# Gate, running sums and scaled level forms made during the odd projection, and the gated scan as a pipeline over heads and levels

## The chip, the cores and the metric

The kernel runs on one core of a Trainium2 chip. The metric is the device time of one execution in microseconds (us). Before the change it was 3591.56 us, the median of three runs (3583.16 to 3595.18).

## The reference, cut to what matters

The program is one inference step of a two-layer decoder trunk for a prompt of 1024 tokens and a group of 8 x 8 sample tokens, 1088 token columns in all. The even layer and the MLPs are not touched. The odd layer is gated linear attention with four heads, key width 128 and value width 256:

```
def gla_mixer(h, s0, w_in, w_a2, b_a, norm_w, w_out):
    q, k, v, r, a1 = _split(h @ w_in, ODD_SPLIT)          # 512, 512, 1024, 1024, 16 columns
    log_a = log_sigmoid(a1 @ w_a2 + b_a) / GATE_TAU
    o, s_new = gated_linear_scan(q * GLA_HK ** -0.5, k, v, log_a, s0)
    o = rmsnorm(o, norm_w) * silu(r)
    return o @ w_out, s_new

# per token: S_t = diag(exp(log_f_t)) S_{t-1} + k_t^T v_t,  o_t = q_t S_t
```

Within a chunk of 128 tokens the score of query t and key s is the sum over the key width of q_t k_s exp(b_t - b_s), where b is the running sum of log_a from the start of the chunk.

## The kernel before

Activations lie with the model dimension on the 128 partitions and the tokens in the free dimension, so a tile is [128, 1088]; the token columns are worked on in three chunks of 384, 352 and 352. The stages of the odd layer follow one another with a barrier between them: `project_stage("odd")`, `alpha_stage`, `scan_stage("gla")`, `project_stage("oddout")`.

**The projection** (`project_stage`) makes 3088 output columns in 25 groups, 24 of 128 and the last of 16. Input and weights are split into a high and a low part, and each product is three matmuls (L96 to L98), so a group is 3 chunks x 8 tiles x 3 = 72 matmuls. For each group SyncE loads the weights (L406), ACT makes the high part (L443), POOL the low part (L516), PE sums, DVE evacuates each chunk with the norm's factor (L493), and SyncE stores the group to the memory tensor `projections` (L410). Two buffers of each kind are used in turn: the load of group g waits for the split of group g-2, and the matmuls of group g for the evacuation of group g-2.

**The alpha stage** loads the 16 gate rows again, multiplies them by `w_alpha2` on PE (L2144), adds the bias on ACT (L2153) and stores four heads of gate logits.

**The scan** (`scan_stage`, here with `hgrn` false) works on the heads one after the other; parts of head h+1 that don't use PE overlap with head h. exp(b_t - b_s) is split over eight levels: level 0 is the diagonal of a chunk, and level 1 to 7 are the pairs in blocks of 2 to 128 tokens, whose query lies in the second half of the block and whose key in the first. For each head:

- `gates` and `running_sum`: Abs, Sigmoid, Ln on ACT (L2379 to L2383), minimum and sum, scaling by 1/16 and the scan over the tokens on DVE (L2493, L2496, L2504). `decayed_forms` makes q exp(b) and k exp(b_last - b) on ACT and DVE.
- `prepare` scales q on POOL (L2326). `differences` forms b minus its value at the middle of each block for every level, on POOL (L2336), ACT takes the exponentials (`decays`, L2412 and L2413), and DVE multiplies the halves by k and q (`scale`, L2539 and L2541). Two buffers `dec` and two `x` are used in turn.
- `scores` on PE multiplies each form with itself for 8 chunks (L2662) and, for the first four levels, the sample tokens (L2665). `keep` on DVE copies the masked scores from PSUM into `a` (two instructions of 512 columns, L2551, and one for the samples, L2554).
- `turn_values` and `turn` transpose v and the decayed k on PE (L2634); ACT copies them out.
- `tail` on PE: the state products of a chunk (`gla_U`, L2699), with the chain of states on DVE (L2576), the values (L2686, L2688), the sample values (L2709, L2712), eight state updates of the samples (L2731, with DVE's L2586) and six matmuls for the mean of squares (L2719). ACT copies and squares the output (L2429, L2430) and makes the norm's factor (L2435, L2438); DVE normalises (L2595) and applies the gate (L2600), and SyncE stores (L2289).

PE's order within the loop over pairs of heads is `turn_values`, `scores`, `tail`, head by head. All loads and stores of the scan are on SyncE's queue.

**The mixed stage** of the even layer (prefix `mix_`, from about 540 to 1110 us) is not changed. It already runs a scan with forms made on the way and a half-width `keep` (L1946) between steps of another attention.

Of the kernel before, what the change touches and what calls it, by code (L numbers as in the profile page):

```python
# [23 lines left out]
P = 128  # L24
# [27 lines left out]
G_Q, G_K, G_V, G_R, G_A, G_GATE = 0, 512, 1024, 2048, 3072, 3088  # L52
Z_ROWS = 3600
# [2063 lines left out]
def alpha_stage(nc, K):  # L2117

    with Stage(nc, "alpha") as s:
        a1, w2, bias = s.sb("a1", [GATE_RANK, T]), s.sb("w2", [GATE_RANK, HEADS * P]), s.sb("bias", [P, HEADS])  # L2120
        out = s.sb("out", [P, HEADS, T])
        bank = [[s.ps(f"bank{i}{c}", [P, 512]) for c in range(NC)] for i in range(2)]
        loaded, projected, biased, stored = (s.sem(n) for n in ("loaded", "projected", "biased", "stored"))
        block = s.block()

        @block.sync
        def _(sp):
            sp.dma_start(a1[:], K.z[G_A:G_A + GATE_RANK, :]).then_inc(loaded, 16)
            sp.dma_start(w2[:], K.w_alpha2[0]).then_inc(loaded, 16)
            with nc.allow_non_contiguous_dma(reason="a column of b_alpha for each head, once"):  # L2130
                sp.dma_start(bias[:], K.b_alpha[0].rearrange("(h p) -> p h", p=P)).then_inc(loaded, 16)
            for h in range(HEADS):
                sp.wait_ge(biased, NC * (h + 1))
                sp.dma_start(K.z[G_GATE + h * P:G_GATE + (h + 1) * P, :], out[:, h, :]).then_inc(stored, 16)
            sp.wait_ge(stored, 16 * HEADS)

        @block.tensor
        def _(pe):
            pe.wait_ge(loaded, 48)
            for h in range(HEADS):  # L2140
                for c, (t0, tn) in enumerate(CHUNKS):
                    if h >= 2:
                        pe.wait_ge(biased, NC * (h - 2) + c + 1)
                    pe.matmul(bank[h % 2][c][:, 0:tn], w2[:, h * P:(h + 1) * P], a1[:, t0:t0 + tn],  # L2144
                              start=True, stop=True).then_inc(projected, 1)

        @block.scalar
        def _(act):
            act.wait_ge(loaded, 48)
            for h in range(HEADS):  # L2150
                for c, (t0, tn) in enumerate(CHUNKS):
                    act.wait_ge(projected, NC * h + c + 1)
                    act.activation(out[:, h, t0:t0 + tn], bank[h % 2][c][:, 0:tn], ACT.Identity,  # L2153
                                   bias=bias[:, h:h + 1]).then_inc(biased, 1)


def scan_stage(nc, K, name, hgrn, rows, norm_w, state_in, state_prompt, state_sample, mix):
# [3 lines left out]


# [3 lines left out]


    VC = 1 if hgrn else 2
    V = VC * P
    C = SEQ // P  # L2170
    L = len(LEVELS) + 1
    LS = 4
    UC = 512 // V
    JS = NB * V // 512
    r_q, r_k, r_v, r_g, r_f = rows
    with Stage(nc, name) as s:
        f_raw = s.sb("f_raw", [P, T])
        q, k = s.sb("q", [P, 2, T]), s.sb("k", [P, 2, T])
        v, gate = s.sb("v", [P, VC, T]), s.sb("gate", [P, VC, T])
        soft, logf, b = s.sb("soft", [P, T]), s.sb("logf", [P, T]), s.sb("b", [P, T])  # L2180
        expb = s.sb("expb", [P, T])
        q_dec = s.sb("q_dec", [P, 2, T])
        last_dec = s.sb("last_dec", [P, 2, C + NB])
        k_tok, v_tok = s.sb("k_tok", [P, 2, C + 1, P]), s.sb("v_tok", [P, 2, C + 1, V])
        dec, x = s.sb("dec", [P, 2, T]), s.sb("x", [P, 2, T])
        a = s.sb("a", [P, C + 1, P])
# [61 lines left out]
        def width(li):  # L2248

            return T if li < LS else SEQ  # L2250

# [621 lines left out]
```

## Time and profile before

| what | value |
|---|---|
| median of 3 runs | 3591.56 us |
| the profiled execution, its own time | 3591.02 us |
| span in its profile | 3589.2 us |
| mean granted TensorE clock | 0.942 |
| busy share of PE, DVE, ACT, POOL | 91%, 34%, 28%, 23% |
| DMA, whole span | 297.53 MB, mean 83 GB/s |
| one `projections<-odd_zout` store | 544.0 KB, 3.1 us to landing |
| one `odd_raw` weight load | 512.0 KB, 4.4 us to landing |
| one `gla_v` or `gla_gate` load | 1088.0 KB, 7.7 and 5.1 us to landing |
| one `gla_s` load, one store | 1024.0 KB, 7.6 and 4.4 us to landing |

PE is TensorE's matmuls, PEld its weight loads, DVE is VectorE, ACT ScalarE, POOL GpSimd, SPq SyncE's queue. L12 is line 12 of the kernel. Times of rows are in us from the start of the span, or ns where a mean is given. In the windows view a row has the stretch, its length, then busy time and records of PE, PEld, DVE, ACT and POOL, the granted clock (1.00 is 2.4 GHz, 0.50 is 1.2 GHz), the DMA engines' busy share and the GB/s moved. In a timeline a row has start, length, engine, line, operation, output <- inputs, the output's and input's shape, the number of merged records and, in brackets, the idle time before it and what ended it.

### The profile page before, as it was taken

What the parts mean: (1) busy time and instruction counts of PE and PEld (TensorE: products, weight loads), DVE (VectorE), ACT (ScalarE), POOL (GpSimd) and SP (SyncE); (2) the same over time, 40 slices, a digit from 0 to 9 for tenths busy, and PEclk for the clock granted to TensorE, in tenths of its full rate; (3) what the DMA queues carried; (4) which work ended last, traced back from release to release, by engine and by line L of the source; (5) the groups of instructions that cost most, each with busy time, mean ns of one, the idle gap of its engine ahead of it and who ended that gap; (6) DMA issues with size and microseconds to landing.
All of it is one profiled execution on the core that took longest, in us unless ns stands there. A gap on an engine that the chain in (4) does not pass through costs nothing. (4 is left out here: it accounts for less than half of the span.)

```text
span 3589.2 us, 52446 instructions
## 1 busy us (share of the span) xinstructions
PE 3271.6 (91%) x21119; PEld 2996.0 (83%) x21119; DVE 1234.5 (34%) x2051; ACT 1019.0 (28%) x1656; POOL 808.8 (23%) x424
## 2 busy tenths in 40 slices
PE   7997797999996999999999899958659899999998
PEld 6996454776775989999999899936549899999998
DVE  4111344665553242222222411145652522222223
ACT  4002123555552232222222300043431422222122
POOL 2121002444440222212121221122211212121211
PEclk8998888999997999999999999978779999999999
DMA  4232003566562111111111032232231111111112
GB/s 154 84 99 86 28 12 127 175 211 221 202 241 94 45 38 48 41 47 41 47 41 47 24 108 85 80 125 83 82 121 48 48 47 41 47 45 43 47 41 73
DMA packets 231778, 297.53 MB, mean 83 GB/s; under 512 B 11936, under 2 KB 193632, under 8 KB 231536
## 3 DMA queue, kind: packets, MB, share of 16 engines
q1 hardware_dynamic: 212944, 212.02, 18.4%
q0 software_dynamic: 18720, 83.92, 6.7%
q8 instruction: 81, 1.33, 0.1%
q14 instruction: 33, 0.27, 0.0%
HBM read 241.96 MB, written 53.94 MB: 82 GB/s over the span
## 5 line engine op out<-in xcount | busy, mean ns | idle before, releaser
L662 POOL TENSOR_TENSOR mlp_w_lo<-mlp_raw,mlp_w_hi 128x1024 fp32r<-128x1024 f32 x126 | 302.9, 2404 | 1239.7 <-ACT mlp_w_hi L623 1239.7
L96 PE MATMUL mlp_bank<-mlp_x_hi,mlp_w_hi 128*128 128x352 f32 (+1 forms) x1536 | 504.5, 328 | 13.0 <-DVE mlp_w_lo L344 12.1
L96 PE MATMUL mlp_bank<-mlp_a_hi,mlp_w_hi 128*128 128x352 f32 (+1 forms) x1536 | 502.6, 327 | 0.9 <-DVE mlp_a_lo L689 0.9
L98 PE MATMUL mlp_bank<-mlp_x_hi,mlp_w_lo 128*128 128x352 f32 (+1 forms) x1536 | 503.3, 328 | 0.0
L97 PE MATMUL mlp_bank<-mlp_x_lo,mlp_w_hi 128*128 128x352 f32 (+1 forms) x1536 | 502.9, 327 | 0.0
L98 PE MATMUL mlp_bank<-mlp_a_hi,mlp_w_lo 128*128 128x352 f32 (+1 forms) x1536 | 502.6, 327 | 0.0
L97 PE MATMUL mlp_bank<-mlp_a_lo,mlp_w_hi 128*128 128x352 f32 (+1 forms) x1536 | 502.1, 327 | 0.0
L705 DVE TENSOR_TENSOR xT<-xT,mlp_bank 128x352 f32<-128x352 f32 (+1 forms) x384 | 202.7, 532 | 527.2 <-PE mlp_bank L98 527.2
L623 ACT ACTIVATE mlp_w_hi<-mlp_raw 128x1024 fp32r<-128x1024 f32 x126 | 132.9, 1055 | 645.4 <-PE mlp_bank L98 645.4
L96 PEld LDWEIGHTS mlp_bank<-mlp_x_hi,mlp_w_hi 128*128 128x128 f32 x1536 | 290.0, 189 | 14.1 <-DVE mlp_w_lo L344 12.7
L97 PEld LDWEIGHTS mlp_bank<-mlp_x_lo,mlp_w_hi 128*128 128x128 f32 x1536 | 291.1, 190 | 0.0
L96 PEld LDWEIGHTS mlp_bank<-mlp_a_hi,mlp_w_hi 128*128 128x128 f32 x1536 | 288.4, 188 | 2.0 <-DVE mlp_a_lo L689 2.0
L98 PEld LDWEIGHTS mlp_bank<-mlp_x_hi,mlp_w_lo 128*128 128x128 f32 x1536 | 289.7, 189 | 0.0
L97 PEld LDWEIGHTS mlp_bank<-mlp_a_lo,mlp_w_hi 128*128 128x128 f32 x1536 | 289.3, 188 | 0.0
L98 PEld LDWEIGHTS mlp_bank<-mlp_a_hi,mlp_w_lo 128*128 128x128 f32 x1536 | 288.1, 188 | 0.0
L697 DVE SCALAR_TENSOR_TENSOR mlp_relu<-mlp_bank,mlp_rstd 128x352 f32<-128x352 f32 (+1 forms) x192 | 102.5, 535 | 527.0 <-PE mlp_bank L98 507.6
L631 ACT ACTIVATE mlp_act<-mlp_relu 128x352 f32<-128x352 f32 (+1 forms) x192 | 97.4, 507 | 467.2 <-DVE mlp_relu L697 467.2
L96 PE MATMUL odd_bank<-odd_x_hi,odd_w_hi 128*128 128x352 f32 (+1 forms) x600 | 197.4, 329 | 6.4 <-DVE odd_w_lo L344 5.9
L98 PE MATMUL odd_bank<-odd_x_hi,odd_w_lo 128*128 128x352 f32 (+1 forms) x600 | 196.9, 328 | 0.0
L97 PE MATMUL odd_bank<-odd_x_lo,odd_w_hi 128*128 128x352 f32 (+1 forms) x600 | 196.8, 328 | 0.0
L1482 PE MATMUL mix_KB<-ident,mix_lat 128*128 128x128 f32 x1280 | 161.7, 282 | 22.9 <-ACT mix_keys L1673 10.5
L96 PE MATMUL even_bank<-even_x_hi,even_w_hi 128*128 128x352 f32 (+1 forms) x528 | 173.9, 329 | 6.2 <-DVE even_w_lo L344 5.7
(430 smaller groups left out, 5591.7 us busy)
## 6 DMA issues: line engine op xcount, KB each, us to landing
mlp_raw<-in_w_down SPq DMA_DIRECT2D x64, 512.0 KB, 3.3
mlp_raw<-in_w_up SPq DMA_DIRECT2D x62, 512.0 KB, 4.1
projections<-odd_zout SPq DMA_DIRECT2D x24, 544.0 KB, 3.1
odd_raw<-in_w_in_odd SPq DMA_DIRECT2D x23, 512.0 KB, 4.4
projections<-even_zout SPq DMA_DIRECT2D x21, 544.0 KB, 3.2
even_raw<-in_w_in_even SPq DMA_DIRECT2D x20, 512.0 KB, 4.5
residual<-xT SPq DMA_DIRECT2D x1, 4352.0 KB, 16.3
xT<-projections SPq DMA_DIRECT2D x8, 544.0 KB, 3.9
```

The source lines that it names most:

```text
L96: pe.matmul(out, w_hi, x_hi, start=first, stop=False)
L97: pe.matmul(out, w_hi, x_lo, start=False, stop=False)
L98: return pe.matmul(out, w_lo, x_hi, start=False, stop=last)
L623: act.activation(w_hi[:, t % 2, :], raw[:, t % 2, :], ACT.Copy).then_inc(hi_done, 1)
L631: act.activation(act2[:, m % 2, 0:tn], relu[:, m % 2, 0:tn], ACT.Square).then_inc(squared, 1)
L662: pool.tensor_tensor(w_lo[:, t % 2, :], raw[:, t % 2, :], r32(w_hi[:, t % 2, :]), ALU.subtract).then_inc(lo_done, 1)
L697: dve.scalar_tensor_tensor(out=relu[:, m % 2, 0:tn], in0=bank[u % 2][m % NC][:, 0:tn], scalar=0.0, in1=rstd[:, t0:t0 + tn], op0=ALU.max, o ...
L705: dve.tensor_tensor(K.xT[:, d, t0:t0 + tn], K.xT[:, d, t0:t0 + tn], bank[d % 2][c][:, 0:tn], ALU.add).then_inc(down_out, 1)
L1482: end = pe.transpose(b[:, i * P:(i + 1) * P], latents(step, 2 * side + i // 2)[:, col:col + P], K.ident[:])
```

## The change

`alpha_stage` is gone, and `project_stage("odd")` and `scan_stage` are replaced by two stages that are written out without loops: `odd_stage` and `gla_stage`. `odd_stage` orders the column groups so that the gate rows come third, makes the gate logits, the running sums `b` of all heads and nine forms per head (seven levels, k decayed to the chunk's end, q decayed from its start) while later groups are multiplied, and stores them to a memory tensor `forms`. `gla_stage` reads the forms and interleaves the levels of head p with the values, sample parts and means of head p-1.

```
-        project_stage(nc, K, "odd", K.w_in_odd[0], ODD_COLS, norm=2, z=K.z)
-        alpha_stage(nc, K)
-        scan_stage(nc, K, "gla", False, (G_Q, G_K, G_V, G_R, G_GATE), K.gla_norm[0], K.state_gla[0],
-                   K.gla_prompt, K.gla_sample, K.mix)
+        odd_stage(nc, K)
+        gla_stage(nc, K)
...
+def odd_stage(nc, K):
+    GROUPS = [("R", 0), ("R", 1), ("A", 0), ("R", 2), ("R", 3), ("R", 4)]
+    for h in range(HEADS):
+        GROUPS += [("Q", h), ("K", h), ("V", h)]
+    GROUPS += [("V", i) for i in range(HEADS, 2 * HEADS)] + [("R", i) for i in range(5, 2 * HEADS)]
...
+    ZB, DB = 6, 4
+    FORMS = len(LEVELS) + 2
...
+    def forms_at(g, c):
+        for h in range(HEADS):
+            n = 3 * (g - at["V", h]) + c
+            if 0 <= n < FORMS:
+                return [(h, n)]
+        return []
...
+    def gates_at(g, c):
+        n = 3 * (g - at["Q", 0]) + c - 1
+        return [n] if 0 <= n < HEADS else []
...
+        @block.sync
...
+            first.load(sp, wv[:, :, column(0):column(0) + P])
+            load(1)
+            sp.dma_start(w2[:], K.w_alpha2[0]).then_inc(gate_in, 16)
...
+            sp.dma_start(starts[:], K.c_starts).then_inc(starts_in, 16)
+            for g in range(2, N + 2):
+                if g < N:
+                    sp.wait_ge(lo_done, g - 1)
+                    load(g)
+                for f in forms_of(g - 2):
+                    store_form(*f)
+                store(g - 2)
...
+        @block.scalar
...
+            for g in range(2, N + 1):
+                if g < N:
+                    split_later(g)
+                if g == LOGITS_AFTER + 1:
+                    add_bias()
+                if g == LOGITS_AFTER + 2:
...
+                for f in forms_of(g - 1):
+                    decay(*f)
...
+        @block.vector
...
+            for g in range(N):
+                for c in range(NC):
+                    evacuate(g, c)
+                    for h in gates_at(g, c):
+                        gates(h)
+                    for f in forms_at(g, c):
+                        scale(*f)
...
+        @block.gpsimd
...
+            for g in range(2, N + 1):
+                if g < N:
+                    split(g)
+                for f in forms_of(g - 1):
+                    difference(*f)
...
+        @block.tensor
...
+            for g in range(2, N):
+                group(g)
+                if g == LOGITS_AFTER:
+                    gate_logits()
...
+def gla_stage(nc, K):
+    ITEMS, FB, RB = L + 1, 8, 5
...
+    def slot_of(kind, h):
+        return dict(k=1, v=2, U=4)[kind] if h == 0 else dict(k=5, v=6, U=7)[kind]
...
+        @block.sync
...
+            load_item(0, 0)
+            load_item(0, 1)
+            sp.dma_start(levels[:], K.c_levels).then_inc(const_in, 16)
+            load_item(0, 2)
+            load_turned(0)
+            for i in range(3, FB):
+                load_item(0, i)
+            sp.dma_start(last_dec[:], K.last_dec).then_inc(dec_in, 16)
+            sp.dma_start(own[:], K.c_own).then_inc(const_in, 16)
+            load_queries(0)
+            load_s0(0)
+            load_s0(1)
+            load_gate(0)
+            for p in range(HEADS + 1):
+                for i in range(SLOTS):
...
...
+        @block.tensor
...
+            for p in range(HEADS + 1):
+                for i in range(SLOTS):
+                    if p < HEADS:
+                        level(p, i)
+                    if p and i < 4:
+                        values(p - 1, i)
+                    if p and i == 4:
+                        sample_values(p - 1)
+                    if p < HEADS and i == slot_of("k", p):
+                        turn_keys(p)
+                    if p and i == 5:
+                        sample_updates(p - 1)
+                    if p < HEADS and i == slot_of("v", p):
+                        turn_values(p)
+                    if p and i == 6:
+                        means(p - 1)
+                    if p < HEADS and i == slot_of("U", p):
+                        chunk_states(p)
...
+        @block.vector
...
+            def keep(h, li):
+                dve.wait_ge(paired, L * h + li + 1)
...
+                end = dve.copy_predicated(
+                    a_h[:, 0:C, :].rearrange("p c (n m) -> p c n m", m=2 * d)[:, :, :, d:2 * d],
+                    half(levels[:, li, :], d, True).unsqueeze(1).broadcast_to([P, C, n, d]),
+                    HB[:].rearrange("p c (n m) -> p c n m", m=2 * d)[:, :, :, d:2 * d])
...
+            dve.wait_ge(const_in, 32)
+            dve.wait_ge(dec_in, 16)
...
+            for p in range(HEADS + 1):
+                for i in range(SLOTS):
+                    if p < HEADS:
+                        keep(p, i)
+                    if p < HEADS and i == slot_of("U", p):
+                        states(p)
+                    if p and i == 5:
+                        sample_states(p - 1)
+                    if p >= 2 and i == 0:
+                        normalise(p - 2)
+                    if p >= 2 and i == 1:
+                        apply_gate(p - 2)
```

ACT's branch at `LOGITS_AFTER + 2` takes Abs, Sigmoid and Ln of the four heads, [128, 1088] each. SyncE's loop in the scan loads item i of head p+1 in slot i, and the other inputs of a head in slots 2, 5 and 7. `keep` is as before at level 0, and from level 1 on it takes only the second halves of the blocks. Score matmuls of a level go to one pair of PSUM banks `HB`, and the matmuls of level i+1 wait for the keep of level i (`a_out`). The other PE results go through five banks in a ring, in a fixed order; each is read by ACT or by DVE, and PE waits until the use five before has been read. The sample updates use 32 of the 64 sample rows at a time, so there are four instead of eight; the squares of the two value halves are added on POOL (`sum_squares`), so there are three mean matmuls instead of six. The stores of the states and of the output are issued from POOL's queue. ACT's `gate_silu` and the norm's factor of head p-1 come in slots 6 and 7; the gate of head p-1 is loaded in slot 2 of pass p, behind a wait for the output of head p-2.

## Rows read from the trace of the kernel before

**Rows 1.** the windows view, five stretches

```profile
2065.00:2341.00 276.00, 273.02 (x1656) 272.74 (x1656) 37.38 (x70) 22.62 (x22) 50.88 (x23) 1.00 0.28 88
2341.90:2364.00 22.10, 14.87 (x24) 7.80 (x24) 0.00 (x0) 6.76 (x12) 0.00 (x0) 0.50 0.27 106
2364.00:2676.20 312.20, 213.43 (x1180) 167.26 (x1180) 188.59 (x252) 133.09 (x200) 88.67 (x38) 0.81 0.27 97
800.00:1000.00 200.00, 186.83 (x2052) 141.41 (x2051) 113.14 (x196) 116.57 (x212) 95.70 (x73) 0.97 0.62 217
2372.00:2380.00 8.00, 0.79 (x4) 0.82 (x5) 1.31 (x2) 5.90 (x5) 2.97 (x1) 0.50 1.02 405
```

**Rows 2.** the timeline of SyncE's queue at the stage borders

```profile
2341.93 0.34 SPq L2128 DMA_DIRECT2D alpha_a<-projections  x1
...
2363.97 0.34 SPq L2254 DMA_DIRECT2D gla_levels<-in_c_levels  x1
...
2670.97 0.37 SPq L2289 DMA_DIRECT2D mixed<-gla_o  x1
2676.23 0.93 SPq L332 DMA_DIRECT2D oddout_raw<-in_w_out_odd  x2
```

**Rows 3.** the timeline of PE in the old scan, neighbours of one kind merged

```profile
2400.77 2.05 PE L2662 MATMUL gla_S<-gla_x 128*128 128x128 f32 x16 [1.00 <-DVE gla_x L2541]
2402.74 0.33 PE L2665 MATMUL gla_U<-gla_x 128*64 128x64 f32 x2
2403.00 1.09 PE L2634 MATMUL gla_TB<-ident,gla_soft 128*128 128x128 f32 x8
...
2431.16 0.39 PE L2686 MATMUL gla_S<-gla_a,gla_v_tok 128*128 128x128 f32 x2
2431.38 0.39 PE L2688 MATMUL gla_S<-gla_q_dec,gla_state 128*128 128x128 f32 x2
...
2433.03 0.43 PE L2709 MATMUL gla_SS<-gla_a,gla_v_tok 64*128 64x64 f32 x2
...
2435.28 0.43 PE L2709 MATMUL gla_SS<-gla_a,gla_v_tok 64*128 64x64 f32 x2
...
2444.37 1.45 PE L2719 MATMUL gla_TB<-gla_sq,ones 128*128 128x352 f32 x4
2445.75 1.12 PE L2731 MATMUL gla_U<-gla_v_own,gla_k_tok 64*128 64x512 f32 x2
2446.80 1.45 PE L2719 MATMUL gla_SS<-gla_sq,ones 128*128 128x352 f32 x4
...
2487.01 1.10 PE L2699 MATMUL gla_U<-gla_v_tok,gla_k_tok 128*128 128x256 f32 x4 [1.75 <-DVE gla_a L2551]
2487.95 0.61 PE L2686 MATMUL gla_S<-gla_a,gla_v_tok 128*128 128x128 f32 x4
```

**Rows 4.** groups by line and form (busy us, mean ns | idle before)

```profile
L516 POOL TENSOR_TENSOR odd_w_lo<-odd_raw,odd_w_hi 128x1024 fp32r<-128x1024 f32 x23 | 55.2, 2402 | 239.9 <-ACT odd_w_hi L443 239.9
L2336 POOL TENSOR_TENSOR gla_dec<-gla_b 128x1024 f32<-128x1024 f32 x16 | 31.3, 1959 | 20.7 <-DVE gla_x L2541 20.7
L1928 DVE TENSOR_TENSOR xT<-mix_dec,xT 128x544 f32<-128x544 f32 x12 | 8.6, 717 | 6.5 <-ACT mix_dec L1730 6.5
```

**Rows 5.** the timelines of POOL and DVE at one moment of the scan

```profile
2475.07 4.05 POOL L2343 TENSOR_TENSOR gla_v_own<-gla_v_tok,gla_own 64x2048 f32<-64x2048 f32 x1
...
2475.58 4.09 DVE L2541 TENSOR_TENSOR gla_x<-gla_dec,gla_q 128x512 f32<-128x512 f32 x1
```

**Rows 6.** the mixed stage's keep: ns min/median/max, first and last start

```profile
L1946 DVE COPY_PREDICATED mix_a<-mix_levels,mix_HB x28: 704/746/1332, 656.5 to 1056.1; 128x512 f32<-128x512 int32 x28
```

**Rows 7.** the timeline at the scan's first values and after its last mean

```profile
2379.21 1.94 PE L2634 MATMUL gla_TB<-ident,gla_v 128*128 128x128 f32 x8 [19.36 <-DMA gla_v<-projections]
...
2661.43 1.45 PE L2719 MATMUL gla_SS<-gla_sq,ones 128*128 128x352 f32 x4
...
2665.93 2.61 DVE L2595 SCALAR_TENSOR_TENSOR gla_o<-gla_o,gla_w_norm,gla_rstd 128x1088 f32<-128x1088 f32 x2 [1.08 <-ACT gla_rstd L2438]
```

More of the change, by code:

```diff
@@ L2135, in _, with load, store, store_form @@
-            sp.wait_ge(stored, 16 * HEADS)
+            def load(g):
+                i = g % 2
+                sp.dma_start(raw[:, i, :, 0:cols(g)], wv[:, :, column(g):column(g) + cols(g)]).then_inc(raw_in[i], 16)
+            def store(g):
+                if g == GATE:
+                    return
+                i = place(g) % ZB
+                sp.wait_ge(evacuated, 3 * g + 9)
+                sp.dma_start(K.z[column(g):column(g) + P, :], zout[:, i, :]).then_inc(z_out[i], 16)
+            def store_form(h, n):
+                e = FORMS * h + n
+                sp.wait_ge(form_made, e + 1)
+                sp.dma_start(K.forms[h, n, :, 0:width(n)], form(h, n)[:, 0:width(n)]).then_inc(form_out[e % DB], 16)
@@ L2137, in _ @@
         @block.tensor
         def _(pe):
-            pe.wait_ge(loaded, 48)
-            for h in range(HEADS):
-                for c, (t0, tn) in enumerate(CHUNKS):
[L2142 to L2145, printed above, removed]
+            pe.sem_inc(evacuated, 6)
+            first_two_groups(pe, bank, lambda i: (w_hi[:, i], w_lo[:, i]), x_hi, x_lo, first, xlo_done, summed, norm)
@@ new lines, in group @@
+            def group(g):
+                i, w = g % 2, cols(g)
+                pe.wait_ge(lo_done, g + 1)
+                for c, (t0, tn) in enumerate(CHUNKS):
+                    pe.wait_ge(evacuated, 3 * g + c + 1)
+                    for k in range(KD):
+                        last = mm3(pe, bank[i][c][0:w, 0:tn], w_hi[:, i, k, 0:w], w_lo[:, i, k, 0:w],
+                                   x_hi[:, k, t0:t0 + tn], x_lo[:, k, t0:t0 + tn], k == 0, k == KD - 1)
+                    last.then_inc(summed, 1)
@@ new lines, in value_out @@
+            def value_out(h, part):
+                vc, side = part // 2, part % 2
+                b, t = bank_of(("o", h, part)), slice(side * 512, side * 512 + 512)
+                wait_filled(act, ("o", h, part))
+                if part == 0 and h:
+                    wait_filled(act, ("m", h - 1, NC - 1))
+                if part == 0 and h >= 2:
+                    act.wait_ge(o_stored[h % 2], 16 * VC * (h // 2))
+                act.activation(o[:, h % 2, vc, t], b[:], ACT.Copy).then_inc(o_read, 1)
+                act.activation(sq[:, vc, t], b[:], ACT.Square).then_inc(read_act, 1)
@@ L2591, in outputs @@
-            def outputs(h):
-                wait(dve, "rstd_out", h, 1)
-                wait(dve, "o_out", h, 3)
+                        end = dve.tensor_copy(state[:, 0, :], u)
+                    else:
+                        dve.wait_ge(s_made, C * h + c)
+                        end = dve.scalar_tensor_tensor(out=state[:, c, :], in0=state[:, c - 1, :], scalar=last_dec[:, h, c:c + 1],
+                                                       in1=u, op0=ALU.mult, op1=ALU.add)
+                    end.then_inc(s_made, 1)
```

1066 lines of the change are left out of this document (557 added, 509 removed).

## The prediction

> **What bounds the kernel now.** I read the page first: TensorE (PE) is busy 91% of the span, so most stages can only be shortened on PE. The slices of the page show two places where that fails, the prompt attention and a stretch behind the middle; the change lies in the second. The windows view splits that stretch by stage [rows 1]. The reader sees three things there. The odd projection runs PE at the full clock without a gap: 1656 matmuls are 23 column groups of 72, and 273.02 / 23 = 11.87 us each; DVE and POOL are busy 37 and 51 us of 276. An f32 matmul leaves two records, a projection's only one. The alpha stage lasts 22 us at granted clock 0.50 (1.2 GHz). The gated scan lasts 312 us with PE busy 213 of them at a mean granted clock of 0.81. The SyncE timeline gives the borders to 0.1 us [rows 2]: alpha 2341.93 to 2363.97, 22.0 us; scan 2363.97 to 2676.23, 312.3 us. So at most these 334 us are at stake, and the change puts new work into a projection that has no spare PE time.
>
> **What is removed.** The alpha stage goes as a stage: its loads, its half-clock matmuls and its round trip through memory, **-22.0 us**. In the scan, Abs, Sigmoid, Ln, the running sum, the seven differences, their exponentials and the scaling no longer sit between the score matmuls. Before, each level waited for that loop: the level that starts at 2400.77 has 1.97 us of PE work, and PE idled 1.00 us for `gla_x` before it [rows 3]; the next head's values, states and means could not fill the gap, because PE's order has one head's parts one after the other.
>
> **What is added to the projection.** (1) Twelve gate matmuls, on PE's path. In alpha they kept PE busy 14.87 us at clock 0.50 and ACT 6.76 us, so 1.24 and 0.56 us each [rows 1]; at the full clock 0.62 us. They go through two banks, so a pair costs one matmul, its drain, one bias activation and the waits, about 1.45 us: 6 x 1.45 = 8.7, I take **+9.0** (ends 7.4, the bare matmuls, and 14.9, their old time). (2) The last group is now 128 rows wide where it was 16, so a full store of 0.56 MB stands at the end: **+1.2** (ends 0 and 2). (3) The 12 activations of the gate over whole rows fall in two groups without forms; at most three of the 0.56 each, they take 20.2 of 23.7 us, so the next weight split is in time. (4) Forms: 36 in twelve groups, three each. Per group POOL has the weight split (2.40 us) and three differences (1.96 us at 1024 columns, so 2.0), DVE three pairs of multiplications (2 x 0.72 us at 544 columns [rows 4], less at 512, so 1.38 a pair) and three evacuations (37.38 / 70 = 0.53 us [rows 1]). These two engines don't overlap when both read SBUF: a DVE multiplication of 0.68 us took 4.09 us because POOL's `gla_v_own` of 4.05 us was running, and ended 0.6 us after it [rows 5]. The sum is then 2.4 + 3 x 2.0 + 3 x 1.38 = 12.5 us per group against 11.87 of PE. Walking through it, ACT has to split the next weights between POOL's third difference and POOL's next split, and DVE's work doesn't all fall into that gap: I get 12.8 us. The third group of a head has one difference fewer and makes up 0.7. So POOL falls back by 1 + 1 - 0.7 = 1.3 us a head, 5 us in all; its split is due 8.3 us after the time at which it now ends, so PE hardly waits. I take **+2.0** (ends 0, and 3.1 x 12 - 8 = 29 if nothing overlaps: 15.0 us per group). The form stores add 19.5 MB in 140 us to a DMA share of about 0.3, which leaves room. SyncE now issues three form stores before each z store and next load; a late form delays the load of weights by as much, in the same 8 us of cover.
>
> The Trainium skill, "SBUF — State Buffer", section "SBUF: two separate sides", says that the pair of ports is an exclusive lock for the whole instruction, but that a DVE instruction with fewer than two SBUF inputs (outside the 2-port modes) is free of it. The evacuations, with one PSUM input, would by that rule cost nothing extra, as in my sum; were they held as well, a group would be 14.1 us and the stage some 19 us longer, which is inside the 29 above.
>
> **The scan, rebuilt.** The PE work of a head, from start-to-start times at the full clock [rows 3]: eight levels, four with the sample pair at 2.23 us and four at 1.97, 16.8; 27 transposes at 0.215 (four in under 1.09), 5.8; eight 256-wide state matmuls, 0.94 for two, 3.6; 30 value matmuls at 0.223, 6.7; sample values 2 x 2.25, 4.5; four updates instead of eight at 1.05, 4.2; three means instead of six at 0.69, 2.1. Sum 43.7; the slots add it up to 44.2 with one short wait after the first level. The other engines fit under it: in the old scan a head took 47 us of DVE, 33 of ACT and 22 of POOL [rows 1], and gates, sums, differences, exponentials and scaling, about half of it, are gone. A level's own loop (matmuls, then one half-width keep of 0.75 us and its sample part, then the next level) is 3.3 to 3.8 us. That keep is already in the mixed stage, strided and with PSUM input, at a median of 746 ns [rows 6]; its maximum of 1332 is the upper bound and would still be covered in the middle passes, where a slot has 3.8 to 8.2 us of PE work.
>
> Passes: p = 0 has only levels, transposes and state sums; p = 1 to 3 hold everything; p = 4 is the tail.
> Start: DVE waits for the last decays and the ownership table before its first keep, and those are behind some 6.55 MB on SyncE's queue. Before, PE could use v, with 3.87 MB on the queue, at 2379.21, 15.2 us after the first issue [rows 2, 7]; the other 2.7 MB go at 405 GB/s [rows 1], 6.7 us: 21.9. First keep 1.8. (Ends 19 and 26 for both.)
> p = 0 from level 1: 4.3 (level and 9 key transposes), 6.1 (level and 18 of the values), 3.8 (a level's own loop), 5.6 (level and states), three loops of 3.3, and half of the first slot again for its 1.2 GHz after the idle start, 2: 31.7 (29 to 35).
> p = 1 to 3: 44.2 each if PE never waits; with PE's share of the mixed stage, 186.83 of 200 us [rows 1], 47.5. I take 46.5, nearer the row: 139.5 (132.6 to 150).
> p = 4: values, samples, updates, means 17.5; from the last mean to the normalisation 4.5 less its own 1.4 [rows 7]; silu, which waits for a gate loaded only after the head before it is stored, adds about 0.4; normalise and gate, 2665.93 to 2670.97, 5.04 [rows 2, 7]: 26.0 (25 to 29).
> To the next stage: 5.3 as before [rows 2], and 0.8 because POOL issues the store, which it did not in the old scan (0 to 4): 6.1.
> Sum 21.9 + 1.8 + 31.7 + 139.5 + 26.0 + 6.1 = 227.0 against 312.3: **-85.3 us**.
>
> DMA in a middle pass: 9.27 MB in and 2.29 out, 11.56 MB in 46.5 us, 249 GB/s. The mixed stage held 217 GB/s at a share of 0.62, so 350 at a full one; loads are issued a pass ahead, and I cost them at nothing. Without that cover a pass would be 11.56 / 0.217 = 53 us.
>
> The stores go from SyncE to POOL's queue. The Trainium skill, in the same section of "SBUF — State Buffer", warns that descriptors of such transfers are written by GpSimd, which a 2-port DVE instruction locks out. By it the last store could start up to one 1.3 us multiplication late; no run here shows it yet.
>
> **Total.** -22.0 - 85.3 + 9.0 + 1.2 + 2.0 = -95.1. The profiled execution took 3591.0 us (span 3589.2 and 1.8 around it), the median 3591.6. Prediction: 3591.0 - 95.1 = **3496 us**.
>
> **Rivals.**
> A, the port decides in the projection: 15.0 us per group while forms are made, 29 instead of 2: 3523. For it: the 4.09 us multiplication. Against: the gap in which ACT splits is free for DVE. Chance 0.12.
> B, the middle passes are bound by DMA or by waits between banks: 53 us each, +20: 3516; with the upper ends elsewhere 3535. For it: five ring banks with two readers in fixed order, one queue of loads with many waits. Against: each wait I followed ends at least 0.1 us before PE comes. 0.12.
> C, PE never waits and the start is short: 44.2 per pass, forms free: 3496 - 7 - 2 - 7 = 3480 or less. 0.10.
> D, the other side: PE stays at 1.2 GHz in the scan. Its 175 us would be 350: 3496 + 150 = 3646. The gain is gone once 175 / c = 270, a mean clock of 0.65; over this scan with its gaps it was 0.81, and in the dense mixed stage 0.97 [rows 1], so 0.02.
> E, new waits and contention cancel the gain within 0.3%: 0.01.
> My case, 3480 to 3512: 0.63.
>
> The range is 3474 to 3528: it leaves out D, E, the upper half of B and the lower half of C, 0.14, and of the unknown costs only both ends at once. Changes under 0.3% (11 us) can't be told from none here: faster 0.97, same 0.01 (E), slower 0.02 (D).
>
> **What the profile after would show.** No alpha rows; twelve 16-row matmuls over 9 us in the projection. Group starts 11.9 us apart also while forms are made; if they are 13 or more, A. DVE multiplications of 0.7 that last 2 or more us whenever POOL subtracts. In the scan: first keep 22 us after its first DMA; score levels of one head 45 to 48 us after those of the last; granted clock 0.95 or more in the middle; about 227 us from first DMA to the next stage's. The prediction is wrong if PE's idle time in the middle passes is over 5 us each, if the clock there is under 0.9, or if the projection grows by over 20 us.

## The result, and the profile after

The changed kernel takes **3476.22 us** (median of 4 runs, 3468.98 to 3482.81) against 3591.24 for the one before (median of 4, 3583.16 to 3595.18): ratio 0.9682, 95% interval [0.9656, 0.9708]. The forecast was 3496 in a range of 3474 to 3528. The sign and the range held. The forecast's own case, 3480 to 3512, did not: the gain is 115 us, not 95, and the time lies where rival C put it, which had a chance of 0.10. It lies only 2 us inside the lower end of the range.

The timeline of SyncE's queue in the changed kernel gives the stage borders that answer to [rows 2]: odd projection from 2018.76, scan from 2352.77, next stage from 2559.09.

```profile
2018.76 0.93 SPq L332 DMA_DIRECT2D odd_raw<-in_w_in_odd  x2
...
2352.77 0.81 SPq L2551 DMA_DIRECT2D gla_f<-projections  x2
...
2559.09 0.92 SPq L332 DMA_DIRECT2D oddout_raw<-in_w_out_odd  x2
```

The scan takes 206.3 us where it took 312.3, **-106.0**. The odd projection of before ended at 2341.93 [rows 2]; its start in the same queue:

```profile
2023.41 0.93 SPq L332 DMA_DIRECT2D odd_raw<-in_w_in_odd  x2
```

That is 318.5 us; now it takes 334.0, **+15.5**. The alpha stage is gone, **-22.0**. Upstream, where the code is the same, the trace is 4.7 us shorter; the runs below put the start of the odd projection anywhere from 2014.6 to 2029.5, so this is no part of the change. Downstream +0.5. The sum is -116.7, and the spans (3589.2 and 3472.6) differ by 116.6; the rest is rounding.

The windows view of the changed kernel, the stretches that answer to [rows 1]. Columns: stretch, its length, busy time and instructions of PE, weight loads, DVE, ACT and POOL, granted clock, DMA share, GB/s. In order: the part of the odd projection with forms, the start of the scan, a middle pass, the tail, the whole scan.

```profile
2155.00:2300.00 145.00, 145.00 (x883) 145.00 (x882) 100.90 (x110) 54.01 (x76) 105.35 (x48) 1.00 0.65 229
2352.80:2373.50 20.70, 4.16 (x18) 3.78 (x18) 0.03 (x1) 0.00 (x0) 2.89 (x3) 0.51 0.94 351
2445.00:2486.50 41.50, 40.67 (x297) 36.67 (x296) 20.24 (x34) 16.90 (x26) 7.45 (x7) 0.96 0.79 289
2520.50:2559.00 38.50, 23.45 (x125) 17.91 (x123) 17.76 (x25) 18.67 (x25) 6.14 (x7) 0.72 0.42 145
2352.80:2559.10 206.30, 167.34 (x1156) 149.05 (x1156) 80.06 (x132) 67.71 (x104) 30.77 (x28) 0.86 0.64 228
```

PE is busy for all of the 145 us in which the forms are made, and for 40.67 of 41.5 us in the middle pass, at a granted clock of 0.96. The middle of the scan is now bound by PE. Its ends are not: 20.7 us with 4.16 of PE work at the start, and a tail at clock 0.72.

The four largest waits of PE in that scan (total us, times, longest):

```profile
PE gla_HB L2676 <- DVE gla_a L2857: 13.0, 1, 13.0
PE gla_HB L2676 <- DMA gla_f<-projections: 9.8, 1, 9.8
PE gla_HB L2676 <- DVE gla_a L2862: 3.1, 3, 1.3
PE gla_R L2709 <- ACT gla_rstd L2826: 2.5, 3, 0.8
```

22.8 of these 28.4 us (29.4 with the smaller ones) come before level 1 of the first head. In the middle passes only one kind of wait is left, for the bank that ACT's roots free, 0.83 us a pass; the forecast had no place for it.

The timeline of PE in the changed scan, the lines that answer to [rows 3] (start, us, engine, line, operation, tiles, sizes, count of merged neighbours):

```profile
2402.65 2.02 PE L2676 MATMUL gla_HB<-gla_f 128*128 128x128 f32 x16 [0.91 <-DVE gla_a L2862]
...
2443.32 1.95 PE L2676 MATMUL gla_HB<-gla_f 128*128 128x128 f32 x16
...
2465.43 3.25 PE L2676 MATMUL gla_HB<-gla_f 128*128 128x128 f32 x16
...
2470.01 1.99 PE L2742 MATMUL gla_R<-gla_v_own,gla_k_tok 32*128 32x512 f32 x8
2471.93 2.05 PE L2676 MATMUL gla_HB<-gla_f 128*128 128x128 f32 x16
2473.82 2.13 PE L2699 MATMUL gla_R<-ident,gla_v 128*128 128x128 f32 x18
2475.78 1.99 PE L2749 MATMUL gla_R<-gla_sq,ones 128*128 128x384 f32 x6
2477.61 1.95 PE L2676 MATMUL gla_HB<-gla_f 128*128 128x128 f32 x16
...
2483.95 1.95 PE L2676 MATMUL gla_HB<-gla_f 128*128 128x128 f32 x16
...
2537.22 3.78 PE L2742 MATMUL gla_R<-gla_v_own,gla_k_tok 32*128 32x512 f32 x8
2540.94 3.85 PE L2749 MATMUL gla_R<-gla_sq,ones 128*128 128x384 f32 x6
```

Level 0 of heads 1, 2 and 3 starts 40.7 and 40.6 us apart, where 46.5 was forecast. The prices of a pass can be read from it: 18 transposes in 1.96 us (start to start), four updates in 1.92, three means in 1.83. One line is odd: the level at 2465.43, behind the sample values, takes 3.25 us instead of 1.95. From there to the updates at 2470.01, the level and nine transposes, it is 4.6 us.

### The profile page after: what moved, and what is told of

It is laid out like the page before. It is cut to its first block and busy times, and to the rows that moved or that the text cites. A ratio compares the mean times of both kernels' runs of the same rounds, so it can differ in the third digit from the quotient of the medians.

```text
span 3472.6 us, 51659 instructions
## 1 busy us (share of the span) xinstructions
PE 3224.0 (93%) x21095; PEld 2972.4 (86%) x21095; DVE 1226.2 (35%) x2015; ACT 1010.0 (29%) x1639; POOL 827.1 (24%) x450
## 5 line engine op out<-in xcount | busy, mean ns | idle before, releaser
L96 PE MATMUL odd_bank<-odd_x_hi,odd_w_hi 128*128 128x352 f32 (+3 forms) x600 | 198.3, 331 | 5.9 <-DVE odd_w_lo L344 5.9
L98 PE MATMUL odd_bank<-odd_x_hi,odd_w_lo 128*128 128x352 f32 (+3 forms) x600 | 197.6, 329 | 0.0
L97 PE MATMUL odd_bank<-odd_x_lo,odd_w_hi 128*128 128x352 f32 (+3 forms) x600 | 197.5, 329 | 0.0
L1482 PEld LDWEIGHTS mix_KB<-ident,mix_lat 128*128 128x128 f32 x1280 | 144.2, 144 | 41.6 <-issue 24.4
```

The lines of the kernel that those rows point to most:

```text
L96: pe.matmul(out, w_hi, x_hi, start=first, stop=False)
L97: pe.matmul(out, w_hi, x_lo, start=False, stop=False)
L98: return pe.matmul(out, w_lo, x_hi, start=False, stop=last)
L1482: end = pe.transpose(b[:, i * P:(i + 1) * P], latents(step, 2 * side + i // 2)[:, col:col + P], K.ident[:])
```

## The experiments

All are edits of the changed kernel; its stage times are 334.0 (odd projection) and 206.3 us (scan). The first four, e1_updates, e3_narrow, e4_pool and e5_sequence, were run once each (3474.03, 3469.58, 3492.65 and 3503.90 us) and are read from their traces; the others have five runs each.

**e1_updates: why four updates take 1.92 us and not 4.2.**

```diff
-  pe.matmul(b[:], k_tok[32*g:32*g+32, C, :], v_own[32*g:32*g+32, 2*m:2*m+2, :]...
+  r = {1: slice(0, 32), 2: slice(0, NS)}.get(h, slice(32*g, 32*g+32))
+  pe.matmul(b[:], k_tok[r, C, :], v_own[r, 2*m:2*m+2, :]...
```

> A look at one price, on the changed kernel. The four sample updates of a head took 1.92 us there, 0.48 each, where the prediction said 1.05 each. They have 512 columns and 32 rows, and two that follow each other use rows 0 to 31 and rows 32 to 63. Head 0 stays so. Head 1 takes rows 0 to 31 for all four, head 2 takes all 64 rows for all four (the update values of these two heads are then not the reference's). Theory, two matmuls on different rows of the array run side by side: head 0 1.9 us, head 1 about 3.8, head 2 about 3.8 to 4.2. Rival, half the rows cost half: 1.9, 1.9 and 3.8. Second rival, 1.05 in the old scan was a wait for a bank and not the matmul: 1.9 in all three.

The timeline of PE, the updates of heads 0, 1 and 2:

```profile
2425.82 1.99 PE L2743 MATMUL gla_R<-gla_v_own,gla_k_tok 32*128 32x512 f32 x8
...
2466.42 3.70 PE L2743 MATMUL gla_R<-gla_v_own,gla_k_tok 32*128 32x512 f32 x8
...
2510.38 3.70 PE L2743 MATMUL gla_R<-gla_v_own,gla_k_tok 64*128 64x512 f32 x8
```

1.99 us as changed, 3.70 with all four on rows 0 to 31, 3.70 with all 64 rows. So half the rows cost as much as all, 0.92 each, and the halving comes from neighbours that use different rows: they run side by side. Both rivals fall. The prediction's 1.05 was the price of an update on all 64 rows, one after another; it stood between mean matmuls of 128 rows [rows 3], and what its other 0.13 us were no run isolates.

**e3_narrow: the slow level in each middle pass.**

```diff
-  for bi in range(NB):
+  for bi in [] if h == 1 else range(NB):      # 8-column matmuls of the sample values
```

> In each middle pass of the changed kernel the score level right behind the sample values took 3.56, 3.25 and 2.93 us instead of 1.95, at half clock. Here head 1 leaves out its 16 sample-value matmuls of 8 columns (its sample outputs are not the reference's); heads 0, 2 and 3 keep them. Theory, the clock falls because of these narrow matmuls: the level at that place of the second middle pass takes 1.95 us, the other two stay at 2.9 to 3.6, and that pass is 4.4 + 1.3 = 5.7 us shorter, 34.9 instead of 40.6. Rival, the clock falls for another reason (DMA load, the place in the pass): all three levels stay slow, and the pass is only 4.4 us shorter, 36.2.

The timeline of PE: the level-0 starts, the level behind the place of the sample values in each middle pass, and in the second the updates that follow:

```profile
2401.41 2.02 PE L2676 MATMUL gla_HB<-gla_f 128*128 128x128 f32 x16 [0.91 <-DVE gla_a L2862]
...
2423.59 3.55 PE L2676 MATMUL gla_HB<-gla_f 128*128 128x128 f32 x16
...
2442.11 1.95 PE L2676 MATMUL gla_HB<-gla_f 128*128 128x128 f32 x16
...
2460.74 2.02 PE L2676 MATMUL gla_HB<-gla_f 128*128 128x128 f32 x16 [0.29 <-DVE gla_a L2862]
...
2463.68 1.99 PE L2742 MATMUL gla_R<-gla_v_own,gla_k_tok 32*128 32x512 f32 x8
...
2477.61 1.95 PE L2676 MATMUL gla_HB<-gla_f 128*128 128x128 f32 x16
...
2500.41 3.76 PE L2676 MATMUL gla_HB<-gla_f 128*128 128x128 f32 x16
```

With them 3.55 and 3.76 us, without them 2.02. That pass is 35.5 us long (2442.11 to 2477.61), the one before 40.7. The theory's 34.9 was 0.6 short: the two matmuls of 64 rows stay, so 3.8 us of work are gone and not 4.4, and 0.29 is a wait that the missing work no longer hides. Against that, the half clock costs 1.6 us and not 1.3, since the transposes behind the level run slow too: level and transposes take 4.6 us in each middle pass of the changed kernel and 2.94 here (2460.74 to 2463.68). What the engine did before its clock fell is 16 matmuls of 8 columns (32 records, 4.4 us with the two matmuls of 64 rows); without them it does not fall.

**e4_pool: how much room the forms have.**

```diff
   w, m = width(n), LEVELS[n]
+  if n % 3 == 0:
+      pool.tensor_tensor(extra[:], b[:, h, 0:SEQ], b[:, h, 0:SEQ], ALU.subtract)
```

> How much spare time the forms have in the projection. POOL gets one more subtraction of 1024 columns (about 2 us) in each of the 12 groups with forms, into a tile that nobody reads. In the changed kernel POOL's weight splits in the stretch with forms start 11.67 us apart and PE's groups 11.86, and PE never waits; POOL's 3.1 us of idle time per group is a wait for ACT's half of the split, which is queued behind the last exponential, so it moves with POOL's work. Theory, POOL's loop is as long as PE's group and the 8.3 us of cover are all there is: the splits come 13.5 us apart, POOL falls back by 20 us, and PE waits 10 to 14 us more in the stage (odd stage 344 to 348 instead of 334.0). Rival, POOL has real spare time of 3 us a group: the stage stays at 334. Second rival, the port decides and multiplications stretch as well: 26 us or more.

PE's wait for POOL's split, and SyncE's borders of the odd projection:

```profile
PE odd_bank L96 <- POOL odd_w_lo L2381: 13.0, 10, 1.6
```

```profile
2022.32 0.93 SPq L332 DMA_DIRECT2D odd_raw<-in_w_in_odd  x2
...
2371.75 0.81 SPq L2554 DMA_DIRECT2D gla_f<-projections  x2
```

The stage takes 349.4 us, 15.4 more, of which 13.0 are this wait; the twelve extra subtractions are 26.4 us of POOL. That is the theory's waiting time and 1.4 us over its stage time. The splits of the stretch came 13.4 us apart (13.5 expected). So the forms fit, but with almost nothing over: the loop of split, differences, exponentials and multiplications is as long as PE's group, and of the 26.4 us some 11 were absorbed, near the 8.3 of cover and 0.2 a group.

**e5_sequence: how much is the overlap of heads.** The loops over passes and slots run over the list below; heads all use the slots of head 0.

```diff
-  for p in range(HEADS + 1):      # head p's levels beside head p-1's values
+  PASSES = [x for h in range(HEADS) for x in ((h, None), (None, h))]
+  for new, old in PASSES:         # a head's levels, then its values
```

> Undoes the pipeline over heads and keeps the forms: the changed kernel's parts, but each head's eight levels with its transposes and states run alone, then its values, samples, updates and means alone, then the next head. What it shows is how the 106 us that the scan lost divide between the work moved away and the overlap of heads. Theory, most of it is the work moved away: a head takes 8 level loops of 3.3 to 5.6 us, 30, and 17 us of the rest, 47 instead of 40.6, so the scan is about 22 + 4 x 47 + 18 = 228 us instead of 206, the kernel 3499. Rival, the overlap carries it, because gaps bring the granted clock down to about 0.8 and every level's round trip is open: 60 us a head, scan 270 to 280, the kernel 3545.

The windows view, the whole scan and one head:

```profile
2358.00:2588.00 230.00, 173.51 (x1156) 148.08 (x1156) 80.76 (x132) 67.62 (x104) 32.57 (x28) 0.85 0.58 204
2430.00:2479.00 49.00, 41.86 (x289) 35.75 (x289) 20.56 (x35) 16.73 (x26) 7.50 (x6) 0.93 0.60 213
```

230.0 us against 228 expected: 23.7 more than with the overlap, 49 a head. Of the 106 us that the scan lost, 82 come from what left it (gates, sums, forms, half of the updates and means) with the new order inside a head, and 24 from the overlap of heads; these 82 are not divided further by any run. The rival's 270 falls: the clock stayed at 0.85.

**e2_start: the two small loads in front.**

```diff
   sp.dma_start(levels[:], K.c_levels)...
+  sp.dma_start(own[:], K.c_own)...
+  sp.dma_start(last_dec[:], K.last_dec)...
   load_item(0, 2)
...
-  sp.dma_start(last_dec[:], K.last_dec)...
-  sp.dma_start(own[:], K.c_own)...
```

> Tests the start of the scan. The changed kernel's first keep began 20.7 us after the scan's first transfer, because DVE waited for the ownership table and the last decays, which stand behind eight 0.5 MB loads in SyncE's order; PE idled 13.0 us for it. Here these two small loads are issued right after the level masks. Theory: the first keep begins 9 to 10 us after the first transfer, and since a level's loop of 2.9 to 5.6 us is slower than the landing of its load (0.5 MB at 350 GB/s, 1.5 us), nothing comes late behind it: scan 196 instead of 206.3, kernel 10 us under the changed one. Rival: the first pass is then bound by its loads (the eighth load of the first head stands behind 10.3 MB, 29 us at 350 GB/s), and what is won at the first level comes back as waits for transfers: 0 to 4 us.

SyncE's borders of the scan, and DVE's first keep:

```profile
2352.35 0.81 SPq L2551 DMA_DIRECT2D gla_f<-projections  x2
...
2548.82 0.92 SPq L332 DMA_DIRECT2D oddout_raw<-in_w_out_odd  x2
```

```profile
2361.80 1.33 DVE L2855 COPY_PREDICATED gla_a<-gla_levels,gla_HB 128x512 f32<-128x512 int32 x2 [13.60 <-PE gla_PB L2678]
```

The first keep starts 9.5 us after the first transfer, where it was 20.7, and the scan takes 196.5 us: 9.8 less. No transfer came late behind it. Time: 3468.15 us (5 runs), ratio 0.9665 [0.9646, 0.9685], beside 3474.65 us, 0.9679 [0.9658, 0.9699], for the changed kernel on the same chip. The medians differ by 6.5, and their intervals overlap; the 9.8 are read from the stage.

**e9_after: the changed kernel again**, on that chip.

> The changed kernel itself on the same chip as the other three, so that differences of a few us can be told: 3472 to 3478 us. No theory expects anything else of it.

3474.65 us (3471.13 to 3484.88). Its profile has 334.0 and 206.5 us for the two stages, and a span 10.5 us longer than the first one's; its odd projection began at 2029.49 and not at 2018.76, so the difference lies before it. These two stages repeat to 0.2 us while the kernel's time moves by ten. Over all runs below and above in which a stage's code is unchanged, the projection lies between 333.2 and 334.3 us and the scan between 206.3 and 207.6, so a difference of 1 us in a stage says nothing.

**e6_between: the gate matmuls between the projection's.**

```diff
   for k in range(KD):
       last = mm3(pe, bank[i][c]..., k == 0, k == KD - 1)
+      if g == LOGITS_AFTER + 1 and k % 2:
+          gate_logit((c * KD + k) // 2)
...
   if g == LOGITS_AFTER + 1:
+      split_later(g + 1)
       add_bias()
```

> Tests what the 12 gate matmuls cost. As a block of their own they held the projection up for 13.1 us, and the 13 matmuls behind them ran at half clock, some 1.8 us more, where the prediction had 9.0. Here one stands behind every second step of the sum over k of the next column group, so that bias activations and drains lie beside the projection's matmuls and PE never pauses; ACT makes the next weight split ahead of the biases. Theory: only the bare matmuls are left, 12 x 0.62 = 7.4 us at full clock: odd stage 326.5 instead of 334.0. Rival: the pauses were not drains but the price of switching between the two kinds of matmul, paid 12 times now instead of once: no gain, or up to 5 us longer.

The timeline of PE around one gate matmul and at the start of a later group, and ACT's at the same moment:

```profile
2090.76 0.91 PE L2438 MATMUL odd_sum<-odd_acc,odd_w 16*128 16x384 f32 x2
2091.60 0.44 PE L96 MATMUL odd_bank<-odd_x_hi,odd_w_hi 128*128 128x384 f32 x1
...
2132.34 0.69 PE L96 MATMUL odd_bank<-odd_x_hi,odd_w_hi 128*128 128x384 f32 x1 [6.82 <-POOL odd_w_lo L2381]
```

```profile
2128.83 1.99 ACT L2251 ACTIVATE odd_w_hi<-odd_raw 128x1024 fp32r<-128x1024 f32 x2
```

The stage is 341.0 us, 7.0 longer: a miss of both. One gate matmul holds the row up for 0.94 us (its neighbour before starts at 2090.49, so the next was due at 2090.66 and came at 2091.60) and the one behind it by 0.1, so 1.0 and not 0.62. But the loss is elsewhere: ACT made the split for that group only behind its Abs, Sigmoid and Ln, and PE idled 6.82 us and started at half clock. The order of ACT in this edit made the new wait. Time 3488.75, 0.9722 [0.9702, 0.9741].

**e8_all and e10_best.** e8_all joins e2_start and e6_between with two small edits; e10_best moves that split ahead of Abs.

```diff
-  if p and i == 6: gate_silu(p - 1)
-  if p and i == 7: roots(p - 1)
+  if p and i == (6 if p == HEADS else 7):
+      if p < HEADS: roots(p - 1)
+      gate_silu(p - 1)
+  if p == HEADS and i == 7: roots(p - 1)
...
-  store_o(HEADS - 1)              # POOL's queue; now on SyncE's
...
+  if g == LOGITS_AFTER + 2: split_later(g + 1)       # e10_best alone
```

> The two edits of e2_start and e6_between together, and two small ones: in the middle passes ACT takes the roots of a head before the silu of its gate (PE waited 0.8 us a pass for a bank that the roots free), and the last head's two output stores are issued by SyncE instead of POOL. Theory: -10, -7.4, -2.5 and -0.8, together -20.7 against the changed kernel, about 3455 us. Rival: one of the first two finds its rival, then 3462 to 3466.

> e8_all with its fault mended: ACT makes the split of the second next group's weights (6.8 us of PE idle there, and 1.8 us of matmuls at half clock behind it) ahead of Abs, Sigmoid and Ln, not behind them. Theory: the idle time goes, and what is left of the gate matmuls between the projection's is 12 x 1.0 us (in e6_between each put 1.0 us between its neighbours) instead of 14.9 us for the block: odd stage 331 to 332 instead of 334.0, scan 192.7 as in e8_all, kernel 16 us under the changed one, about 3459. Rival: the split moved ahead delays the gates and then the forms, and the stage's end shows it: 334 or more.

e8_all: 3469.32 us, 0.9666 [0.9645, 0.9687]; its scan is 192.7 us, 3.7 under e2_start's (3.3 expected; PE's wait for the roots' bank is gone), its projection 339.8 with the same 6.8 us wait. That is above the theory's 3455 and above the rival's 3462 to 3466 too, because the gate part that it takes over was worse than either. e10_best: projection 330.2, scan 192.8, 3462.05 us, 0.9642 [0.9627, 0.9657]. The wait is gone and the projection is 3.8 us shorter than with the block; 331 to 332 and 3459 were expected. The last store: from the end of the last gate multiplication to the next stage's first transfer it is 6.2 us with POOL's queue (2552.90 to 2559.09) and 4.0 with SyncE's (e10_best, 2538.09 to 2542.07). The lateness that the prediction feared from the multiplication is at most a small part of this: POOL issued the first of the two stores at 2552.00, while the last multiplication ran, and by the windows view its bytes moved about 1.1 us later, where it was 0.8 us with SyncE's queue. More of it lies behind the last byte: 3.1 us to the next stage's first transfer, and 1.6 with SyncE's.

**e11_pairs: two gate matmuls side by side.**

```diff
+  for r in (0, 32):               # gate weights, and the 16 gate rows by DVE, twice
+      sp.dma_start(w2[r:r + GATE_RANK, :], K.w_alpha2[0])
...
+  for r in (0, 1):
+      h = 2 * (n // NC) + r
+      pe.matmul(logits[r][:, 0:tn], w2[32*r:32*r+GATE_RANK, h*P:(h+1)*P],
+                a1[32*r:32*r+GATE_RANK, t0:t0+tn], start=True, stop=True)
```

> e10_best, and the gate matmuls two at a time on different rows of the array, as the sample updates are: the gate's 16 rows and its weights lie twice, at rows 0 and 32, heads 0 and 1 (then 2 and 3) are computed side by side into the two banks. Theory, from e1_updates (side by side 1.99 us for four, on the same rows 3.70): a pair costs about what one costs now, 6 x 1.0 to 1.2 instead of 12 x 1.0: odd stage 325 to 327, kernel 3453. Rival: the 1.0 us is mostly the change from one kind of matmul to the other and the wait for the bias of the pair before (two activations, 1.15 us), which a pair has twice as large: 330 to 332, no gain.

PE around one pair (four records, two matmuls), the windows view over all six pairs, and SyncE's borders:

```profile
2083.43 0.92 PE L2444 MATMUL odd_sum<-odd_acc,odd_w 16*128 16x384 f32 x4
2084.28 0.45 PE L96 MATMUL odd_bank<-odd_x_hi,odd_w_hi 128*128 128x384 f32 x1
```

```profile
2083.40:2099.00 15.60, 15.60 (x85) 11.41 (x84) 1.61 (x3) 5.10 (x10) 1.60 (x1) 1.00 0.19 55
```

```profile
2016.22 0.93 SPq L332 DMA_DIRECT2D odd_raw<-in_w_in_odd  x2
...
2341.22 0.81 SPq L2559 DMA_DIRECT2D gla_f<-projections  x2
...
2532.12 0.94 SPq L332 DMA_DIRECT2D oddout_raw<-in_w_out_odd  x2
```

A pair takes 0.92 us where one matmul took 0.91, and the clock stays at 1.00. The projection is 325.0 us (325 to 327 expected), the scan 190.9: **3450.02 us** (5 runs, 3445.35 to 3454.33; 3453 expected), ratio 0.9613 [0.9598, 0.9628] against before. It beats both kernels: its interval lies below the changed kernel's. Its scan has the code of e10_best's, and is 1.9 us shorter because PE waited 10.2 and not 12.5 us for the first form; this part is no gain of the pairs.

The Trainium skill, "TensorEngine Tiling (Array Packing)", section "Tiling Modes", under "Key Properties", says that tiles on different rows load and multiply in parallel, and that a change of tiling mode drains the engine. The trace agrees with the first: pairs at the price of one. With the second it does not disagree: a gate matmul holds the row up for 1.0 us, where half of its time in the alpha stage is 0.62. That the extra 0.4 is this drain no run isolates.

## Why the prediction was right, and where it was off

**Alpha, right.** -22.0 forecast, no row of it left.

**Gate matmuls, +9.0, too low.** The windows view of the changed kernel, the block and the 4 us behind it:

```profile
2084.00:2097.00 13.00, 12.86 (x25) 6.16 (x24) 0.53 (x1) 6.15 (x11) 0.00 (x0) 0.62 0.27 83
2097.00:2101.00 4.00, 4.00 (x14) 3.98 (x14) 0.00 (x0) 3.88 (x5) 2.30 (x1) 0.53 0.00 0
```

The block ran from 2083.99 to 2097.02, 13.0 us (within its bounds of 7.4 and 14.9), 2.2 a pair instead of 1.45. The sum had it at full clock; the granted clock was 0.62, since after 3 us of the block it fell to its lower level of 1.2 GHz. It still was 0.53 behind the block, where the next 12 matmuls of 384 columns took 3.9 us (2097.02 to 2100.92) instead of 2.1, another 1.8: this term was in no sum. The **last store, +1.2, was right**: from PE's last matmul to the next stage's first transfer it was 3.83 us before (2338.10 to 2341.93) and is 5.05 now (2347.72 to 2352.77). A wait of 0.5 us for POOL's split in the old projection is gone. 13.0 + 1.8 + 1.2 - 0.5 is all of the +15.5.

**Forms, +2.0, was zero.** The mechanism was right. The timelines of POOL (its first and last weight split in the stretch with forms, and two differences) and of DVE in the changed projection:

```profile
2163.17 2.39 POOL L2380 TENSOR_TENSOR odd_w_lo<-odd_raw,odd_w_hi 128x1024 fp32r<-128x1024 f32 x1 [2.28 <-ACT odd_w_hi L2251]
...
2167.99 4.81 POOL L2397 TENSOR_TENSOR odd_sq<-odd_b 128x1024 f32<-128x1024 f32 x2
...
2303.21 2.40 POOL L2380 TENSOR_TENSOR odd_w_lo<-odd_raw,odd_w_hi 128x1024 fp32r<-128x1024 f32 x1 [5.33 <-ACT odd_w_hi L2251]
```

```profile
2162.46 0.72 DVE L2365 TENSOR_TENSOR odd_sq<-odd_sq,odd_zout 128x544 f32<-128x544 f32 x1
...
2163.53 2.62 DVE L2364 TENSOR_TENSOR odd_sq_pool<-odd_sq_pool,odd_zout 128x544 f32<-128x544 f32 x1
...
2168.54 0.55 DVE L2332 SCALAR_TENSOR_TENSOR odd_zout<-odd_bank,odd_rstd 128x384 f32<-128x384 f32 x1
```

A multiplication of 0.72 us takes 2.62 while POOL subtracts, as forecast, and the evacuation at 2168.54, which runs beside POOL's subtraction, takes 0.55. Twelve intervals between splits lie there, 11.67 us each, and PE's groups are 11.87 [rows 1]. The sum had 12.8; it seems to have laid DVE's work behind POOL's where part of it fits into the time in which ACT makes the exponentials and the split, but no run isolates this. e4_pool shows how near the end of the cover was.

The Trainium skill, "SBUF — State Buffer", section "SBUF: two separate sides", frees an instruction with one SBUF input from the lock, and this trace agrees: with POOL subtracting beside it the evacuation takes 0.55 us, and the 19 evacuations of 352 columns of this kind from 2155 to 2300 us have a mean of 0.51.

**Scan, -85.3, was -106.0.** By the prediction's own steps: start 20.7 (21.9 forecast), first keep 1.6 (1.8), pass 0 27.6 (31.7), passes 1 to 3 121.9 (139.5), tail 28.3 (26.0), to the next stage 6.2 (6.1). The term that was mis-sized most is **the PE work of a head, 43.7 us**, and the choice of 46.5 comes on top:
- "27 transposes at 0.215 (four in under 1.09)". A transpose leaves one record, so the x8 of [rows 3] are eight transposes, not four: 0.11 to 0.12 each, 3.0 us (1.96 for 18, 1.08 for nine at full clock in e3_narrow) and not 5.8. I had read the count as two records each, as for other f32 matmuls. -2.8 a head.
- "four updates instead of eight at 1.05": 1.92 and not 4.2. The edit that halved their number also put them on different rows, which the prediction overlooked (e1_updates). -2.3.
- Means 1.83 and not 2.1, -0.3. That leaves 38.3, and the other parts, some a little shorter and some longer, 38.2. The wait of 0.83 for the roots' bank and 1.6 of half clock behind the sample values (e3_narrow), both put at nothing, make the 40.6 to 40.7 that were measured.
- "I take 46.5, nearer the row": the old mixed stage's 93% of PE was not this loop's, which has 98%. The two choices for caution, this (2.3 a pass, 6.9) and the 2.0 above, cost 9 us; the prices of transposes, updates and means cost 16 over three passes.

Pass 0 has the same 27 transposes: the 18 of the values take 2.0 us there where the sum had 3.9. The tail was 2.3 us longer. PE's part of it took 20.2 us and not 17.5, because the clock fell to half within the second set of sample values: these took 5.9 us (4.5 in the sum), updates and means 3.7 and 3.9 (4.2 and 2.1 in the sum, but 1.92 and 1.83 at full clock). The start's mechanism (constants behind 6.5 MB of loads) was right, and e2_start shows that it was no need: two small loads moved ahead take 9.8 us off.

**The rivals.** A (port) fell: POOL never came late. B fell: the middle passes moved up to 289 GB/s and PE waited 0.8 us each. C's time came, 3476 for its "3480 or less", and its free forms, but not its passes: PE does wait, 0.83 us each, the start is only 1 us under the forecast, the gate block cost 6 us more, and the passes are 40.6 where C had 44.2. D fell: clock 0.86 in the scan. E fell. C was given 0.10 because its passes of 44.2 were the least that the sum allowed; with the prices above, three passes would have been 16 us shorter, and my own case would have been about 3480, an estimate.

**How much was luck.** The stages miss by +3.3 (projection) and -20.7 (scan), and 4 us of the rest lie upstream, where nothing was changed. Errors of both signs and these 4 us together left the profiled execution (3474.4) and the median (3476.2) just inside 3474; the signs by which the prediction would have been wrong were all avoided: 0.83 us of idle time in a middle pass, clock 0.96 there, and a projection longer by 15.5 us against a limit of 20. "45 to 48" us between heads and "about 227" for the scan did not come. Three slips in its working don't matter to the result: 44.2 at PE's share of 186.83 in 200 is 47.3 and not 47.5, four times 0.94 is 3.8 and not 3.6, and the 15.0 us per group of rival A stands without a working.

**Not tried:** the tail with its squares summed in parts, so that means need not wait for the sample values; and a second gate buffer.

## What to carry to other kernels

Before pricing an instruction by its rows, find out how many records one leaves, and see whether neighbours use the same rows of the array: two oversights of this kind put 5.1 us too much into each pass. When work is moved under another engine's cover, measure the cover by adding to it (12 more subtractions cost 15 us here), since a stage with no wait can be one operation away from one. And look for the small load behind large ones: 10 us of the first pass hung on the place of two short transfers in a queue.

## What the runs showed of the hardware that was not expected

- f32 matmuls of 512 columns cost 0.92 us with 32 or 64 rows, and 0.48 where neighbours use rows 0 to 31 and 32 to 63; with 16 rows and 384 columns a pair takes 0.92, one 0.91.
- The granted clock fell to half for about 3 us behind 16 f32 matmuls of 8 columns, with PE busy all the time; without those it did not (2.02 against 3.55 and 3.76 us for the same level). In the tail, where updates of 32 rows and means follow them, it stayed at about half to the end of PE's work (0.53 from 2537 to 2545 us).
- A block of 12 f32 matmuls of 16 rows, with short waits for a bank, was at full clock for 3 us and at half for the other 10; the same matmuls in pairs between those of the projection left the clock at 1.00 (e11_pairs).
- An f32 matmul of 16 rows between 128-row ones held the row up for 1.0 us; half of its time in the alpha stage (at half clock, 1.24 us) is 0.62.
